# The recurrence's block inverse in two halves, one bank for all turns, weights' low halves on GpSimd

## What is computed

```python
def step(S, inp):
    r_t, w_t, k_t, v_t, kk_t, kka_t = inp
    sa = jnp.einsum('bhvk,bhk->bhv', S, kk_t)
    S = (S * w_t[:, :, None, :]
         - sa[..., None] * kka_t[:, :, None, :]
         + v_t[..., None] * k_t[:, :, None, :])
    y_t = jnp.einsum('bhvk,bhk->bhv', S, r_t)
    return S, y_t
...
k = xk @ w_in[1]
v = xv @ w_in[2]
w_log = -jax.nn.softplus(-(w0 + jnp.tanh(xw @ w1) @ w2).astype(f32)) - 0.5
a = jax.nn.sigmoid((a0 + (xa @ a1) @ a2).astype(f32))
```

## Time and profile before

| | |
|---|---|
| median of 3 runs | 2123.78 us (2120.54 to 2123.8) |
| the profiled execution | 2121.93 us, its span 2120.2 us |
| TensorE busy | 1949.6 us, 92% |
| VectorE busy | 1265.2 us, 60% |
| ScalarE busy | 881.7 us, 42% |
| GpSimd busy | 69.5 us, 3% |
| mean granted TensorE clock | 0.968 |
| recurrence, first scores of the first and of the last step | 275.0 and 853.5 us |

### The profile page before, as it was taken

How to read it: one execution, slowest core, us unless ns; L and a number is a source line. 1 busy time by engine, 2 the same in 40 slices (tenths; PEclk the granted TensorE clock), 3 DMA queues, 4 the chain that set the end, 5 groups by cost and what they waited for, 6 DMA issues and landing times.

```text
span 2120.2 us, 43501 instructions
## 1 busy us (share of the span) xinstructions
PE 1949.6 (92%) x18926; PEld 1506.4 (71%) x18926; DVE 1265.2 (60%) x1871; ACT 881.7 (42%) x1297; POOL 69.5 (3%) x102
## 2 busy tenths in 40 slices
PE   4999799999999999689999999999887599999997
PEld 2677566766766676478888888887765378888885
DVE  5572177777777777554555545455556667778532
ACT  3242245545546455343322222345336555444321
POOL 2000000000000000000000000000001000000000
PEclk8999999999999999889999999999998699999998
DMA  3224310111111100053222222332110032333331
GB/s 112 72 90 134 102 53 29 40 44 40 34 39 40 43 29 19 2 167 103 100 95 95 99 100 94 95 100 71 59 35 26 10 99 93 98 100 99 92 91 67
DMA packets 50444, 154.12 MB, mean 73 GB/s; under 512 B 8401, under 2 KB 10705, under 8 KB 49745
## 3 DMA queue, kind: packets, MB, share of 16 engines
q1 hardware_dynamic: 50112, 149.26, 21.9%
q10 hardware_dynamic: 144, 2.10, 0.3%
HBM read 145.04 MB, written 6.29 MB: 71 GB/s over the span
## 4 chain that ended last, share of the span: by engine, by line
PE 50%; DVE 3%; ACT 2%; issue 1%; POOL 0%; DMA 0%; POOLq 0%; ACTq 0%; DVEq 0%
PE bank L1398 15%; PE bank L1399 15%; PE bank L1397 15%; PE bank L1485 1%; PE bank L1486 1%; PE bank L1487 1%; PE bank L1522 0%; DVE room L2115 0%; DVE room L2082 0%; PE bank L1505 0%; PE bank L1566 0%; PE bank L1557 0%; PE bank L1468 0%; PE bank L1533 0%; PE bank L1530 0%
## 5 line engine op out<-in xcount | busy, mean ns | idle before, releaser
L1604 ACT ACTIVATE w_hi<-raw 128x1024 fp32r<-128x1024 f32 (+2 forms) x200 | 202.9, 1015 | 516.5 <-PE bank L1399 467.5
L1397 PE MATMUL bank<-h_hi,w_hi 128*128 128x512 f32 x896 | 349.9, 391 | 0.0
L1398 PE MATMUL bank<-h_lo,w_hi 128*128 128x512 f32 x896 | 348.6, 389 | 0.0
L1399 PE MATMUL bank<-h_hi,w_lo 128*128 128x512 f32 x896 | 348.6, 389 | 0.0
L148 DVE TENSOR_TENSOR w_lo<-raw,w_hi 128x1024 fp32r<-128x1024 f32 (+2 forms) x200 | 234.3, 1173 | 166.7 <-ACT w_hi L1604 166.1
L1397 PEld LDWEIGHTS bank<-h_hi,w_hi 128*128 128x128 f32 x896 | 168.2, 188 | 35.8 <-issue 0.7
L1398 PEld LDWEIGHTS bank<-h_lo,w_hi 128*128 128x128 f32 x896 | 168.2, 188 | 35.4 <-issue 0.7
L1399 PEld LDWEIGHTS bank<-h_hi,w_lo 128*128 128x128 f32 x896 | 168.2, 188 | 35.0
L141 PE MATMUL bank<-xg_hi,g_hi 128*128 128x512 f32 x256 | 103.3, 403 | 26.4 <-DVE xg_lo L148 18.3
L1397 PE MATMUL bank<-y_hi,w_hi 128*128 128x512 f32 x256 | 101.0, 394 | 12.9 <-DVE y_lo L148 12.9
L670 ACT ACTIVATE swapT<-invT 64x256 f32<-64x256 f32 x160 | 66.4, 415 | 106.1 <-DVE invT L1129 57.5
(11 more groups left out here) (360 smaller groups left out, 4095.9 us busy)
## 6 DMA issues: line engine op xcount, KB each, us to landing
raw<-in_w_conv SPq DMA_DIRECT2D x64, 512.0 KB, 3.2
raw<-in_w_up SPq DMA_DIRECT2D x44, 512.0 KB, 3.2
raw<-in_w_out SPq DMA_DIRECT2D x32, 512.0 KB, 3.8
raw<-in_w_in SPq DMA_DIRECT2D x20, 512.0 KB, 3.3
g_raw<-in_w_g SPq DMA_DIRECT2D x16, 512.0 KB, 3.3
g_raw<-in_w_r SPq DMA_DIRECT2D x16, 512.0 KB, 3.9
w_k<-in_w_k SPq DMA_DIRECT2D x16, 512.0 KB, 3.3
w_v<-in_w_v SPq DMA_DIRECT2D x16, 512.0 KB, 3.5
```

Source lines behind the costliest of these rows:

```text
L1397: pe.matmul(to, whi, hi, start=begin, stop=False)
L1398: pe.matmul(to, whi, lo, start=False, stop=False)
L1399: last = pe.matmul(to, wlo, hi, start=False, stop=end)
L1604: act.activation(w_hi[:, g % RING, 0:width], raw[:, g % RAW, 0:width], ACT.Copy).then_inc(S("whi"), 1)
```

## The change

The four blocks are divided into two halves `a` (blocks 0 and 1, blocks 2 and 3). Each half has two banks of its own (4 and 5, 6 and 7) for scores and level products. The masks, sums, transposes and swaps of a level become two instructions of half the size, one for each half. All turns and the mixed values now go through bank `GV`, and the variances through bank `GK`; so a turn waits for ScalarE's copy of the turn before. The low parts of the weights are made on GpSimd, a whole 128x1024 at a time, but for the first of k and of v, which stay on VectorE. The order of all queues is written anew: the low-rank products go to the start of a step, the two tanh with them, `exps` and `decay` to level 3, `reads`, `decayed_keys`, `removed_keys` and `removals` ahead of the group norm's end, and fewer values matmuls stand between the key parts and the phi products (8 in place of 12, and 14 at the step's end). In the prologue ScalarE makes the high part of v behind both tanh, and `bonus_sums` comes after the dense values.

```diff
-        ROT = bank[4:6]
-        X = bank[6:8]
+        X = lambda a, h: bank[4 + 2 * a + h]
+        ROT = bank[6:8]
...
-            def step(c, p=None):
-                q = c % 2 if p is None else p
-                if not (isinstance(c, int) and c == IC - 1):
-                    prepare(c + 1, 1 - q)
-                    chunk_ends(c + 1, 1 - q)
+            def split(n, name):
+                pool.wait_ge(S("whi_" + name), n + 1)
+                split_lo(pool, wts[name][1][:, :], raw[name][:, :], wts[name][0][:, :]).then_inc(S("wlo_" + name), 1)
...
             prepare(0, 0)
+            split(1, "k")
             chunk_ends(0, 0)
-            run(step)(pool)
+            for c in range(IC - 1):
+                split(c + 1, "v")
+                prepare(c + 1, (c + 1) % 2)
+                if c < IC - 2:
+                    split(c + 2, "k")
+                chunk_ends(c + 1, (c + 1) % 2)
...
+                if not last:
+                    tanh_decay(c + 1, 1 - q)
+                swaps(0)
+                if not last:
+                    tanh_rate(c + 1, 1 - q)
+                swaps(1)
                 turned(c, 0)
-                swapped(c, 1)
-                swapped(c, 2)
+                swaps(2)
                 turned(c, 1)
                 if not last:
                     keys(c + 1, 1 - q)
-                swapped(c, 3)
+                swaps(3)
                 turned(c, 2)
                 if not last:
-                    tanh_decay(c + 1, 1 - q)
+                    exps(c + 1)
                 turned(c, 3)
+                swaps(4)
                 if not first:
                     outputs(c - 1)
-                swapped(c, 4)
-                if not last:
-                    tanh_rate(c + 1, 1 - q)
...
             def turn(c, k):
-                if k < 2:
-                    pe.wait_ge(S("mk"), 2 * c + k + 1)
+                if k:
+                    pe.wait_ge(S("turned"), 4 * c + k)
+                elif c < IC - 1:
+                    pe.wait_ge(S("tanh_a"), c + 2)
...
+                for a in range(2):
+                    if a:
+                        need(pe, S("phi"), 2 * c)
+                        need(pe, S("rh"), c)
+                    apart(pe)
+                    scores(bet, 0, q, a)
+                    scores(kd, half, q, a).then_inc(S("mk_mm"), 1)
+                if not last:
+                    low_rank(c + 1, 0)
+                fill(keys, 10)
+
+                lows(0)
                 states(1)
+                if not last:
+                    low_rank(c + 1, 1)
+                ups(0)
                 states(2)
+                fill(keys, 4)
+
+                lows(1)
+                states(3)
+                fill(keys, 2)
+                ups(1)
+                states(4)
                 turn(c, 0)
                 fill(keys, 3)
+                lows(2)
+                states(5)
+                fill(keys, 2)
+                ups(2)
+                states(6)
+                turn(c, 1)
                 fill(keys, 3)
+                lows(3)
+                states(7)
                 turn(c, 2)
+                ups(3)
+                turn(c, 3)
                 if not last:
                     key_sums(c + 1)
-                low_products(c, 4)
+                lows(4)
                 mixed_values(c)
-                up_products(c, 4)
+                ups(4)
...
+                masked(LA, 0, 0, "mk_mm", "la")
+                masked(MK, half, 0, "mk_mm", "mk")
+                masked(LA, 0, 1, "mk_mm", "la")
+                for a in range(2):
+                    dve.wait_ge(S("la"), 2 * c + a + 1)
+                    dve.tensor_tensor(invT[:, of(a), :, :], LA[:, :, of(a), 0, :].rearrange("p h b k -> p b h k"),
+                                      over2(C["level_first"]), ALU.mult).then_inc(S("inv0"), 1)
+                for a in range(2):
+                    dve.wait_ge(S("inv0"), 4 * c + a + 1)
+                    dve.tensor_tensor(flat(invT, a), flat(invT, a), over(C["eye"], 4), ALU.add).then_inc(S("inv0"), 1)
+                for a in range(2):
+                    dve.wait_ge(S("inv0"), 4 * c + 3 + a)
+                    dve.transpose(flat(inv, a), flat(invT, a)).then_inc(S("inv"), 1)
+                masked(MK, half, 1, "mk_mm", "mk")
```

More of the change, by code:

```diff
@@ L726, in _ @@
             exps(0)
-            split(1, "k")
             values(0)
             split(1, "v")
-            run(step)(act)
+            for c in range(IC):
+                step(c)
             outputs(IC - 1)
@@ L778, in bonus_sums, with scores @@
                 pe.wait_ge(S("bon"), n + 1)
+                need(pe, S("yln"), n - 1)
                 pe.matmul(GK[:, :], C["head_sum"], bon[:, :], start=True, stop=True).then_inc(S("bsum_mm"), 1)
-            def scores(lhs, out, q):
-                for b in range(TB):
+            def scores(lhs, at, q, a):
+                for b in range(2):
                     for k, src in enumerate((kap[:, :], rt[:, q, :])):
@@ new lines, in up_products @@
+            def up_products(c, lv, a):
+                pe.wait_ge(S("low"), 2 * (LV * c + lv) + a + 1)
+                pe.wait_ge(S("swap"), 4 * (LV * c + lv) + 2 * a + 2)
+                apart(pe)
+                for b in (2 * a, 2 * a + 1):
+                    for h in range(2):
+                        for j in range(2):
+                            right = invT[rows[j], b, 0, :] if h == 0 else swapT[rows[1 - j], b, :]
+                            m = pe.matmul(X(a, h)[rows[j], cols(2 + b % 2)], low[rows[j ^ h], b, h, :], right,
+                                          start=True, stop=True)
+                m.then_inc(S("up_mm"), 1)
@@ new lines, in key_parts @@
+            def key_parts(c, a):
+                if a == 0:
+                    pe.wait_ge(S("mv"), c + 1)
+                pe.wait_ge(S("inv"), inv_count(c, LV, a))
+                apart(pe)
+                for h in range(2):
+                    for b in (2 * a, 2 * a + 1):
+                        for j in range(2):
+                            m = pe.matmul(X(a, h)[rows[j], b % 2 * P:(b % 2 + 1) * P], invT[rows[j], b, h, :],
+                                          XK[rows[j], b, h, :], start=True, stop=True)
+                m.then_inc(S("tkg_mm"), 1)
@@ L855, in chain, with step @@
                     m.then_inc(S("y_mm"), 1)
[L857 to L860 removed]
+            def step(c):
+                last, first, q = c == IC - 1, c == 0, c % 2
                 keys = iter(()) if last else dense(c + 1, "k", GK)
@@ L979, in step @@
                 fill(values, 24)
+            low_rank(0, 0)
             for _ in dense(0, "k", GK):
                 pass
-            low_rank(0, 0)
+            low_rank(0, 1)
             key_sums(0)
-            low_rank(0, 1)
-            bonus_sums(0)
             for _ in dense(0, "v", GV):
                 pass
-            run(step)(pe)
+            bonus_sums(0)
+            for c in range(IC):
+                step(c)
             for i in range(1, NCH):
@@ L1092, in state, with step @@
                     .then_inc(S("st"), 1)
-            both = lambda t: t.rearrange("p h b k -> p (h b) k")
-            def step(c, p=None):
-                q = c % 2 if p is None else p
-                last = isinstance(c, int) and c == IC - 1
-                first = isinstance(c, int) and c == 0
+            def step(c):
+                last, first, q = c == IC - 1, c == 0, c % 2
                 def states(i):
@@ L1142, in step @@
                 states(4)
-                if not last:
-                    split(c + 1, "v", 0, 2)
                 added(1)
+                turned(1)
                 states(5)
@@ L1148, in step @@
                 states(6)
-                if not last:
-                    split(c + 1, "v", 1, 2)
                 added(2)
+                turned(2)
                 states(7)
                 masked_low(3)
+                if not last:
+                    decay(c + 1)
                 added(3)
+                turned(3)
+                if not last:
+                    key_factor(c + 1)
                 masked_low(4)
@@ L1177, in step @@
                 if not last:
-                    reads(c + 1, 1 - q)
-                    removed_keys(c + 1)
-                    removals(c + 1)
-                    decayed_keys(c + 1)
-                if more(c):
-                    split(c + 2, "k", 0, 1)
-                if not last:
                     bonuses(c + 1, 1 - q)
-            split(0, "k", 0, 1)
-            split(0, "v", 0, 2)
-            split(0, "v", 1, 2)
             channels(0, 0)
+            first_split("k")
+            decay(0)
+            first_split("v")
             clamp(0)
-            decay(0)
             key_factor(0)
             bonus_products(0, 0)
+            reads(0, 0)
+            decayed_keys(0)
             normed(0)
             rated(0)
-            reads(0, 0)
             removed_keys(0)
             removals(0)
```

(5 more changed lines are left out.)

257 lines of the change are left out of this document (102 added, 155 removed).

## The result

The changed kernel takes 2149.09 us (median of 4 runs, 2147.12 to 2153.6), the one before 2122.16 us (the median of four runs, one more than in the table of before): a ratio of 1.0131, with a 95% interval of 1.011 to 1.0152. It is slower, and the forecast was 2154 (2128 to 2170). The profiled execution took 2148.47 us, its span 2146.7.

A forecast was written before the change was run, and what follows sets the result against it. TensorE was taken as the bound. Fourteen steps at 2.35 us more, +2, -1.3 and -3 give +31 on the profiled 2121.9; with half the 1.9 gap to the median, 2154 us, range 2128 to 2170 (8 in 10).

The forecast's parts named there:

- Start of a step: First scores matmul to last key matmul: scores no longer wait, and the last key matmul ends at 18.6 us.
- The exclusion: At a step's start, GpSimd's split of v and then ld hold VectorE's level_first chain: 1.55 us a step.
- my prices: TensorE issue times assumed per kind of work, such as 0.23 us for a dense matmul and 0.41 for a turn.
- the k split: GpSimd's split for k, behind the NTG copies, can hold yn for 2.7 us, hidden by later need.
- From the last key matmul to the phi products: This stretch takes 14.5 us, set by ScalarE's unbroken queue of 14.1 us; TensorE's own work is 10.8.
- To the next scores: Phi products to next scores: 7.6 us against 6.5 before, with six more values matmuls and no wait for bet.
- The whole step: A full recurrence step takes 40.7 us against 38.4 by the same prices, 2.35 us more.
- the two named costs: VectorE held beside GpSimd at a step's start, and ScalarE's single queue after the last key matmul.
- Once each: Terms outside the full steps: first step +2 us, prologue 1.3 earlier, last step -3.
- Sum: Whole kernel: 14 x 2.35 + 2 - 1.3 - 3 = +31 us.
- The page on GpSimd: Skill's 4497 ns for 2048 elements, halved to 2.25 us for the split, gives about 2146; not adopted.
- The faster rival: At level 3's up products: ScalarE's run hidden and level_first not held, step 35.5 us, near 2075; half-way 2100; chance 0.12.

The follow-up runs named there:

- e1: Changed kernel with GpSimd's split of the v weights delayed until both eye sums of the step are done: 2134.02 us, ratio 1.0049.
- e4: Changed kernel with the weights' low halves back on VectorE, nothing else changed: 2138.37 us, ratio 1.0063.
- e2: Changed kernel with ScalarE's swaps of level 3 ahead of turn 1's copy and the keys: 2136.52 us, ratio 1.0064.
- e10: Changed kernel with only 12 values matmuls in place of 8 between the key parts and the phi products: 2137.85 us, ratio 1.0075.
- e3: Changed kernel with the edits of e1 and e2 together: 2119.82 us, ratio 0.9987 to the kernel before.
- e8: e3 with 12 values matmuls in place of 8 between the key parts and the phi products: 2104.23 us, ratio 0.9914 to the kernel before.
- e6: e3 with exps behind the NTG copies and reads, removed_keys, removals, decayed_keys behind rated: 2114.73 us, ratio 0.9963 to the kernel before.
- e9: e8 with exps behind the NTG copies and VectorE's reads, removed_keys, removals, decayed_keys behind rated: 2112.97 us, ratio 0.9959 to the kernel before.

## Why the prediction was right, point by point

- *Start of a step.* Scores and keys wait no longer: right. The last key matmul was to end 18.6 behind the scores; it ended at 18.53. That it is so close is luck: two terms in that sum were off and cancelled. The exclusion was put at 1.55 and is 1.1 (e1: 18.53 to 17.39). Its course was right: the first `level_first` stands until GpSimd's split ends, and the second stands beside `ld`, 0.4 longer than by itself. What was mis-sized is the split, 2.37 and not 2.8, which is the whole difference. And without the exclusion I had 17.05 where e1 shows 17.39. In e1's trace TensorE waits for nothing from the scores to the last key matmul, so this is its own issue time, which my prices put 0.3 too low; which of them, no run separates. The second half's low products would have come at 6.1 by my count; in e1 they go together with the first half's, from 5.57 on.
- *Place and nature of the exclusion.* Two `level_first` with a mean of 0.905, beside a GpSimd subtraction, while LA and MK pass: right, and shown by moving the split (e1) and by taking it away (e4). On the k split the step was right in the price and wrong in the name: 2.3 us at the step's end, hidden, but it hit the copy of `affine` and not `yn`. That it is hidden shows in e4, which has no split on GpSimd: from the phi products to the next scores there are 7.51 us, as in the changed kernel (7.49, medians of the steps).
- *From the last key matmul to the phi products.* Forecast 14.5, measured 14.60; ScalarE's work there 14.1, measured 13.92; first up products of level 3 waiting 1.4, measured 1.18; swaps of 64x128 at 0.31, measured 0.308. e2 and e10 show from both sides that ScalarE's run sets this stretch.
- *To the next scores.* 7.6, measured 7.48 (422.51 to 429.99).
- *The whole step.* +2.35 forecast, +2.14 measured (40.62 against 38.48), and e3, level with the kernel before, shows that the two named costs are the whole net loss. From the second scores to the last ones that is 29.7 us in the traces (forecast 32.9); the last step's first scores are at 852.7 in the trace of before, not at 853.5 as the table has it, and at 879.6 in the changed kernel's.
- *Once each.* Three small terms. The last step's levels stand 2.87 apart where they took 3.92, right, as TensorE's timeline of the changed kernel shows:

```profile
888.59 0.79 PE L825 MATMUL bank<-inv,LA 64*64 64x64 f32 x32 [0.57 <-DVE inv L1137]
...
891.46 0.79 PE L825 MATMUL bank<-inv,LA 64*64 64x64 f32 x32 [0.18 <-DVE inv L1137]
```

But from the last step's first scores to the first `y_hi` behind the recurrence only 1.3 us is won (51.8 against 53.1), not 3. The first step is 0.2 longer, not 2; its two `level_first` take the normal 0.42 each, so it doesn't have that cost. The first scores of all come at 272.0 in place of 275.0, 3.0 earlier and not 1.3; but the same prologue gave anything from 269.1 to 274.2 in the experiments' traces, so this term can't be told to better than 2 us. Together -4.1 against the -2.3 forecast.
- *Sum.* 29.7 - 4.1 is 25.6 us up to the end of the recurrence; the profiled executions differ by 26.5.
- *The page on GpSimd.* The estimate of 2.25 us for the split from the Trainium skill (GPSIMD Engine Reference, section 3.1) was nearer to the measured 2.37 than my 2.8 from a row of half the size. The sum with it was 2146; the median is 2149. The measured 2.37 in the same place of my sum would give 0.43 us a step less than the 2.8, about 2148.

The faster rival had the right place. It asked for a ScalarE run that is hidden; that is not what the change does, but the edits e2 and e8 come near to it, and with e1 they give the time that the new order can have. That leaves 2104, not the 2075 that I gave for a step without any wait: 37.57 us a step and not 35.5. In e8 the fourth turn, the variances and the key parts still wait 0.39, 0.45 and 0.25 us a step for ScalarE. The other 1.0 is TensorE's own issue time beyond my prices, 0.35 up to the last key matmul and 0.65 behind it.

## What to carry to other kernels

Work moved to an idle engine isn't free when that engine and the one it was taken from exclude each other: look which instructions of the loaded engine stand beside it and beside what follows it in its queue, and put the moved work where that engine reads PSUM. When an order is written anew, add up each engine's unbroken run between two of its waits; here the run on ScalarE, busy for only 43% of the span, set a third of each step, and moving four short copies into one of its pauses won 1.1 us a step. When a wait stays that can't be shortened, move independent matmuls into it from where they cover nothing.

## What was not expected of the hardware

- A copy of 128x2 elements with one input in SBUF, 0.16 us by itself, took a mean of 2.04 us beside GpSimd's split (15 of them; 0.162 where GpSimd has no split). I had expected this only of instructions with two inputs in SBUF. The Trainium skill (SBUF — State Buffer, "Who interferes with whom") counts copies among the instructions that can hold and want the shared ports; the trace agrees. In e1 the transposes, and the masks and scalings that read PSUM, passed beside the split without delay.
- GpSimd's time for two inputs isn't in proportion to the row that I used: 1.48 us for 511 elements, 2.37 to 2.40 for 1024 (2.52 for the split of k in e6 and e9, beside `kd`).
- `ld` on GpSimd, 0.62 us by itself, holds VectorE as the split does: the second `level_first` takes 0.83 beside it in the changed kernel, and in e4, where I had not expected it, the second `eye` takes 0.84; 0.42 is normal. `ld` itself grows to a mean of 0.69 and 0.82. In both traces it starts during the VectorE instruction before, and the next one ends about 0.3 us behind it, so they seem to take turns, the earlier one first.
